# A three-layer network kernel on one core: the idle products at the stage seams are taken out

## The chip, the core and the metric

The kernel runs on one core of a Trainium2 chip. The engines are named as the profile names them: PE is TensorE (the products), DVE is VectorE, ACT is ScalarE, POOL is GpSimd, SP is SyncE, which issues most DMAs. The metric is the device time of one execution in microseconds.

## What is computed

One sequence of 512 tokens with 1024 features goes through three layers in float32:

```
x = x + ssd_gla_layer(rms_norm(x)); x = x + swiglu(rms_norm(x))     # layer 1: state space mixer and gated linear attention
x = x + mla_layer(rms_norm(x));     x = x + swiglu(rms_norm(x))     # layer 2: latent attention
h = rmsnorm(x)                                                      # layer 3
x = x + (sigmoid(gate_a) * (o_hg @ w_branch_hg) + sigmoid(gate_b) * (o_ret @ w_branch_ret)) @ w_out
x = x + peer_ffn(rmsnorm(x))                                        # 8 heads choose 16 of 16384 experts for each token
return rmsnorm(x)
```

`swiglu` is `(silu(h @ w_gate) * (h @ w_up)) @ w_down` with 2816 hidden features. `o_hg` and `o_ret` are the outputs of a gated recurrence (HGRN2) and of a retention layer. `peer_ffn` scores all experts by product keys, and adds `g * gelu(u_e . x) * v_e` for each chosen expert.

## The kernel before, in words

The work is one long row of stages, and in nearly all of them PE multiplies a weight matrix by the activations. Activations lie transposed in SBUF as 8 tiles of 128 features by 512 tokens (`c.xT`). Float32 precision is had from three products: each operand is split in a high half in the faster format `F32R` and a low half, the rest. ACT makes the high half by a copy, DVE or POOL the low half by a subtraction, and `passes` (L430 to L434) does high by high, high by low and low by high. Weights come in pieces of 128 by 1024 through a ring of two slots (four in the expert stage): SP loads, ACT writes `w_hi`, POOL writes `w_lo`, PE uses it. Every engine has its own instruction order, and semaphores with counted values tie them (`Tally`).

A stage is written in a block of its own, or shares one with its neighbour. At the end of a block the engines meet; PE then waits until DVE has opened the next stage (the semaphore increment at L661 in `linear_block`, at L2085 in `swiglu`). Such a place is called a seam here. Most seams hold a root mean square norm: PE sums squares (`root`, L290 on, uses the sum), ACT takes the logarithm and the exponential, and in the next stage the class `Normal` (L307 on) makes the eight parts of the normalised activations in turn. DVE multiplies (L357), ACT copies the high half (L337), and DVE (L362, parts 0, 1, 2, 4, 6) or POOL (L348, parts 3, 5, 7) makes the low half. POOL also splits one weight piece in front of them (L344). PE takes part k when its low half is there (`normal.ready`): three products a part where one output tile is made at a time (`linear_block`), six where two are made together (`swiglu` at L2068 and `first_latents` at L2349 on), two in the first pass of the expert stage (L3465, L3466).

At these seams the kernel has idle products. They multiply a constant by a constant into a bank of PSUM that is overwritten at once, and nobody waits for them:

```
285 def occupy(c, pe, bank, n):
287     for _ in range(n):
288         pe.matmul(c.ps[:, bank, 0:3 * P], c.ident, c.basic[:, 0:3 * P], start=True, stop=True)
```

They stand at the start of a stage with a norm or with halves of its own to make (L646, L2068, L2349, L3517: three each), at the end of a token-major layer (`linear_tokens`, L795: three), before the last sum of squares in `direct_attention` (L1726: four), behind two layers of 16 output tiles (L651, through the argument `rest`: four each), and before the expert sums (L3570: six). Over the run these are 63 products. In the seams behind the two layers with `rest` they are followed by the next stage's three.

The last stage (`peer_stream`, L3073 on) has two halves. In the first, 128 pieces of expert inputs are multiplied by the activations (L3465 to L3469), and meanwhile DVE and POOL treat the gates. In the second, `add(n, i)` adds 128 pieces of expert outputs: for each piece SP loads weights and two inputs (L3183, L3203, L3205), ACT and DVE make the halves of the multiplied weights (L3379, L3699; L3695 multiplies) and of the expert rows (L3275, L3704), and PE does 18 products into six banks. DVE also adds the first 128 tokens' own rows (L3713), which POOL gathers (L3418).

Of the kernel before, what the change touches and what calls it, by code (L numbers as in the profile page):

```python
# [283 lines left out]

def occupy(c, pe, bank, n):

    for _ in range(n):
        pe.matmul(c.ps[:, bank, 0:3 * P], c.ident, c.basic[:, 0:3 * P], start=True, stop=True)

def root(c, act, width):
# [93 lines left out]
def first_pieces(w):  # L385

    return [w[m, :, :] for m in range(min(2, w.shape[0]))]
# [49 lines left out]
def linear(c, w, kt, nb, hi, lo, dst, add=False, src=None, then=None, beside=None, root_of=None, normal=None,  # L437
           width=D, more=None, ends=None, loads=(), rest=0, whole=None, run=None, head=True, tail=True, tokens_next=False):

    with ExitStack() as ctx:
        linear_block(c, ctx, w, kt, nb, hi, lo, dst, add, src, then, beside, root_of,
                     Normal(c, ctx, normal, width, whole, ends, (hi, lo)) if normal else None, more, loads, rest,
                     run, head, tail, tokens_next)
# [6 lines left out]

def linear_block(c, ctx, w, kt, nb, hi, lo, dst, add, src, then, beside, root_of, normal, more, extra=(), rest=0,
                 run=None, head=True, tail=True, tokens_next=False):
# [49 lines left out]
    with opened(c, run) as block:  # L507
# [112 lines left out]
        @block.tensor  # L620
        def _(pe):
            if head:
                pe.sem_inc(c.piece_free.sem, 2)

            def one(i, r, q, m, s, first=False):
                pe.wait_ge(c.lo_done.sem, c.lo_done.at(3) + m)
                if q == 0:

                    pe.wait_ge(c.bank_free.sem, c.bank_free.at(1) + i)
                if not head and q == 1 and m == 1:  # L630
                    pe.wait_ge(c.bank_free.sem, c.bank_free.at(2))
                for k in range(pt):
                    at = slice(k * P, (k + 1) * P)
                    if first and normal:
                        normal.ready(pe, k)
                    elif first:

                        pe.wait_ge(c.dve_done.sem, c.dve_done.at(k + 1))
                    mm = passes(pe, c.ps[:, r, :], half(c.w_hi, s)[:, at], half(c.w_lo, s)[:, at],
                                hi(q * pt + k), lo(q * pt + k), q == 0 and k == 0, q == np_ - 1 and k == pt - 1)  # L640
                mm.then_inc(c.piece_free.sem, 1)
                if more:
                    more[1](pe, i)
            if src or normal:
                pe.wait_ge(c.bank_free.sem, c.bank_free.at(1))
                occupy(c, pe, 0, 3)  # L646
                one(0, 0, 0, 0, 0, first=True)
            pieces(one, None if root_of or more else pe.Fori, 1 if src or normal else 0)
            if rest:
                pe.wait_ge(c.bank_free.sem, c.bank_free.at(1 + nb))  # L650
                occupy(c, pe, nb % 2, rest)  # L651
            if root_of:
                pe.wait_ge(squares_added.sem, squares_added.at(nb - 2))
                pe.matmul(c.ps[:, RS, :], c.ones, square_sum[:], start=True, stop=False)
                pe.wait_ge(c.squared.sem, c.squared.at(nb))
                pe.matmul(c.ps[:, RS, :], c.ones, sq[:, (nb - 1) % 4, :], start=False, stop=True).then_inc(c.summed.sem, 1)
# [51 lines left out]
def linear_tokens(c, w, kt, nb, hi, lo, dst, beside=None, run=None, head=True):  # L708
# [29 lines left out]
    with opened(c, run) as block:  # L738
# [35 lines left out]
        def _(pe):  # L774
# [19 lines left out]
            pe.wait_ge(c.bank_free.sem, c.bank_free.at(1 + nb * NCH))  # L794
            occupy(c, pe, 4 * flip, 3)  # L795

# [840 lines left out]
def direct_attention(c, x, v, out, gate, then):  # L1637
# [7 lines left out]
    with ExitStack() as ctx:  # L1645
# [8 lines left out]
        with nc.Block() as block:  # L1654
# [7 lines left out]
            def _(pe):  # L1662
# [55 lines left out]
                for h in range(H):  # L1718
# [5 lines left out]
                    if h:  # L1724
                        sum_squares(h - 1)
                occupy(c, pe, 3, 4)  # L1726
                sum_squares(H - 1)
# [238 lines left out]
def swiglu(c, layer, then):  # L1966
# [11 lines left out]
    with c.nc.Block() as run, ExitStack() as ctx:  # L1978
        hid_hi = c.sb(ctx, f"hid_hi{layer}", [P, HT, T], F32R)
        hid_lo = c.sb(ctx, f"hid_lo{layer}", [P, HT, T], F32R)  # L1980
        with ExitStack() as inner:
# [3 lines left out]
            with nullcontext(run) as block:  # L1985
# [64 lines left out]
                def _(pe):  # L2050
# [16 lines left out]
                    pe.wait_ge(c.bank_free.sem, c.bank_free.at(1))  # L2067
                    occupy(c, pe, 0, 3)  # L2068
                    for k in range(DT):
# [52 lines left out]
def latent_attention(c, then):  # L2122
# [15 lines left out]
    with ExitStack() as ctx:  # L2138
# [44 lines left out]
        with nc.Block() as block:  # L2183
# [43 lines left out]
            def _(pe):  # L2227
# [120 lines left out]
                def first_latents():  # L2348
                    occupy(c, pe, 0, 3)  # L2349
                    pe.wait_ge(c.lo_done.sem, split_at(0))  # L2350
# [575 lines left out]
def mix2(c):  # L2926
# [3 lines left out]
    with ExitStack() as outer:  # L2930
# [39 lines left out]
        with ExitStack() as ctx:  # L2970
# [10 lines left out]
            with ExitStack() as inner:  # L2981
                g = c.sb(inner, "g_ret", [P, 16, T])
                gated = GatedNorm(c, inner, lambda t: qk[:, t, :], lambda t: g[:, t, :])
                linear(c, d["w_ret_g"], DT, 16, hh, hl, g, beside=(gated.vector, gated.scalar),
                       more=(lambda sp, m: None, gated.tensor, gated.gpsimd), then=first_pieces(d["w_branch_ret0"]),
                       rest=4)
                gated.close()
            y_ret = c.sb(ctx, "y_ret", [P, DT, T])
            with ExitStack() as inner:
# [11 lines left out]
            linear(c, d["w_gates"], DT, 16, hh, hl, qk, beside=(merge.vector, merge.scalar), then=first_pieces(d["w_out_2"]),  # L3001
                   rest=4, run=block, head=False)
            run.close()
# [69 lines left out]
def peer_stream(c, hh, hl, out):  # L3073
# [6 lines left out]
    with ExitStack() as ctx:  # L3080
# [86 lines left out]
        with nc.Block() as block:  # L3167
# [287 lines left out]
            def _(pe):  # L3455
# [50 lines left out]
                def gates(g):  # L3506
# [9 lines left out]
                    mm.then_inc(gate_mm.sem, 1)  # L3516
                occupy(c, pe, 0, 3)  # L3517
                for m in range(NQ):
# [35 lines left out]
                def add(n, i, first=False):  # L3554
# [14 lines left out]
                    mm.then_inc(c.mm_done.sem, 1)  # L3569
                occupy(c, pe, SUM_BANK[0], 6)  # L3570
                for i in range(4):
# [323 lines left out]
```

## Time and profile before

| | us |
|---|---|
| median of 3 runs | 3753.21 (3751.49 to 3753.91) |
| the profiled execution | 3751.39 |
| its span, from first to last instruction | 3749.2 |

The profile is one execution. The trace gives each instruction's start and length; the length of a product contains a tail in which the next one already runs, so the distance of two starts tells what one costs.
### The profile page before, as it was taken

Reading aid. Unit: us, or ns where it says so; the run is one execution under the profiler, and the core shown is the slowest. Engines: PE = TensorE matmul, PEld = TensorE weight load, DVE = VectorE, ACT = ScalarE, POOL = GpSimd, SP = SyncE. Lnnn points to the kernel's source line nnn. Section 1 sums busy time; section 2 is a strip of 40 time slices with the busy share of each in tenths; the row PEclk is TensorE's granted clock in tenths of the full one; section 3 lists DMA queues with packets and bytes.
Section 4 is the critical chain, followed back from the end, with each engine's and each line's share of the span. In section 5 each row is a group of like instructions: output and inputs, shape, how many; then the busy total and the mean of one; then the engine's idle time right before and its main releaser. Section 6 shows DMA issues by size and latency. Waiting matters only on the chain. (4 is left out here: it accounts for less than half of the span.)

```text
span 3749.2 us, 50283 instructions
## 1 busy us (share of the span) xinstructions
PE 3610.9 (96%) x17367; PEld 2990.4 (80%) x17367; DVE 1963.0 (52%) x3524; ACT 1384.3 (37%) x2161; POOL 1624.1 (43%) x838
## 2 busy tenths in 40 slices
PE   8899899998999999998899999999999999999999
PEld 6668678886677888787687777779999999888887
DVE  6825333204653330227516122458899992788777
ACT  3333332224653222231221332333348994333333
POOL 4444354344105444441344344445786776342221
PEclk9999999999999999999999999999999999999999
DMA  5122132222002222230132122224778997999997
GB/s 172 34 92 92 43 98 95 95 96 83 23 23 97 95 90 94 84 95 23 42 115 85 51 79 85 90 99 142 267 244 298 380 378 288 364 361 357 344 343 254
DMA packets 275168, 580.19 MB, mean 155 GB/s; under 512 B 119712, under 2 KB 153888, under 8 KB 273616
## 3 DMA queue, kind: packets, MB, share of 16 engines
q1 hardware_dynamic: 238160, 444.07, 35.9%
q0 software_dynamic: 36864, 134.23, 10.1%
q8 instruction: 87, 1.43, 0.2%
q14 instruction: 57, 0.47, 0.0%
HBM read 523.66 MB, written 54.56 MB: 154 GB/s over the span
## 5 line engine op out<-in xcount | busy, mean ns | idle before, releaser
L432 PE MATMUL ps<-h_hi,w_hi 128*128 128x512 f32 x1880 | 744.3, 396 | 21.3 <-DVE h_lo L362 11.0
L433 PE MATMUL ps<-h_lo,w_hi 128*128 128x512 f32 x1880 | 736.5, 392 | 0.0
L434 PE MATMUL ps<-h_hi,w_lo 128*128 128x512 f32 x1880 | 736.4, 392 | 0.0
L594 POOL TENSOR_TENSOR w_lo<-ring,w_hi 128x1024 fp32r<-128x1024 f32 (+1 forms) x173 | 445.9, 2578 | 637.0 <-ACT w_hi L559 637.0
L559 ACT CAST w_hi<-ring 128x1024 fp32r<-128x1024 f32 (+1 forms) x173 | 191.5, 1107 | 734.5 <-PE ps L434 728.9
L432 PEld LDWEIGHTS ps<-h_hi,w_hi 128*128 128x128 f32 x1880 | 355.8, 189 | 112.3 <-DVE h_lo L362 15.4
L3414 POOL TENSOR_TENSOR w_lo<-ring,w_hi 128x1024 fp32r<-128x1024 f32 x142 | 359.1, 2533 | 151.6 <-ACT w_hi L3275 150.5
L434 PEld LDWEIGHTS ps<-h_hi,w_lo 128*128 128x128 f32 x1880 | 355.8, 189 | 75.0
L433 PEld LDWEIGHTS ps<-h_lo,w_hi 128*128 128x128 f32 x1880 | 355.8, 189 | 74.9 <-issue 2.2
L3275 ACT CAST w_hi<-ring 128x1024 fp32r<-128x1024 f32 x270 | 282.2, 1045 | 351.7 <-PE ps L434 269.0
L3465 PE MATMUL ps<-h_hi,w_hi 128*128 128x384 f32 (+1 forms) x1152 | 399.9, 347 | 3.8 <-DVE h_lo L362 3.1
L3466 PE MATMUL ps<-h_lo,w_hi 128*128 128x384 f32 (+1 forms) x1152 | 394.7, 343 | 0.0
L3418 POOL DMA_INDIRECT xT<-in_expert_v,row_index x128 | 150.0, 1172 | 377.7 <-DVE ps L3713 363.1
L432 PE MATMUL ps<-w_hi,one_hots 128*128 128x512 f32 x768 | 303.8, 396 | 1.1 <-DVE one_hots L3699 1.1
L434 PE MATMUL ps<-w_hi,one_hots 128*128 128x512 f32 x768 | 303.4, 395 | 0.0
L433 PE MATMUL ps<-w_lo,one_hots 128*128 128x512 f32 x768 | 303.4, 395 | 0.0
L2035 POOL TENSOR_TENSOR w_lo<-ring,w_hi 128x1024 fp32r<-128x1024 f32 x84 | 201.9, 2404 | 227.6 <-ACT w_hi L2008 227.5
L675 DVE TENSOR_TENSOR xT<-xT,ps 128x512 f32 x48 | 33.0, 687 | 383.4 <-PE ps L434 383.4
L3469 PE MATMUL ps<-h_hi,w_lo 128*128 128x384 f32 (+1 forms) x1152 | 230.6, 341 | 1.8 <-POOL w_lo L3414 1.8
L3465 PEld LDWEIGHTS ps<-h_hi,w_hi 128*128 128x128 f32 x1152 | 217.6, 189 | 11.7 <-DVE h_lo L362 4.0
L3466 PEld LDWEIGHTS ps<-h_lo,w_hi 128*128 128x128 f32 x1152 | 218.0, 189 | 4.5
L3469 PEld LDWEIGHTS ps<-h_hi,w_lo 128*128 128x128 f32 x1152 | 203.9, 188 | 7.7 <-POOL w_lo L3414 2.5
(430 smaller groups left out, 6661.3 us busy)
## 6 DMA issues: line engine op xcount, KB each, us to landing
ring<-in_expert_u SPq DMA_DIRECT2D x128, 512.0 KB, 4.8
ring<-in_expert_v SPq DMA_DIRECT2D x128, 512.0 KB, 5.9
ring<-in_w_gate_up SPq DMA_DIRECT2D x88, 512.0 KB, 3.6
acts<-expert_gelu SPq DMA_DIRECT2D x128, 192.0 KB, 4.2
gates<-peer_region SPq DMA_DIRECT2D x48, 512.0 KB, 8.1
peer_region<-acts SPq DMA_DIRECT2D x128, 192.0 KB, 4.8
peer_region<-gates SPq DMA_DIRECT2D x128, 192.0 KB, 5.8
ring<-in_w_down SPq DMA_DIRECT2D x32, 704.0 KB, 4.1
```

Of the source, the lines that this page charges most:

```text
L432: pe.matmul(out, w_hi, x_hi, start=start, stop=False)
L433: pe.matmul(out, w_hi, x_lo, start=False, stop=False)
L434: return pe.matmul(out, w_lo, x_hi, start=False, stop=stop)
L559: act.copy(half(c.w_hi, s), raw(s)).then_inc(c.hi_done.sem, 1)
L594: pool.tensor_tensor(half(c.w_lo, s), raw(s), half(c.w_hi, s).bitcast(F32), ALU.subtract).then_inc(c.lo_done.sem, 1)
L2035: pool.tensor_tensor(c.w_lo[:, at], c.ring[:, u * SLOT:u * SLOT + D], c.w_hi[:, at].bitcast(F32), ALU.subtract).then_inc(c.lo_done.sem, 1)
L3275: act.copy(at_slot(c.w_hi, i), at_slot(c.ring, i)).then_inc(c.hi_done.sem, 1)
L3414: pool.tensor_tensor(at_slot(c.w_lo, i), at_slot(c.ring, i), at_slot(c.w_hi, i).bitcast(F32), ALU.subtract).then_inc(c.lo_done.sem, 1)
L3418: pool.indirect_dma_start(rows[:, j % 4, :], None, table, bass.IndirectOffsetOnAxis(ap=row_at[:, j:j + 1], axis=0)).then_inc(row_loaded[j ...
L3465: pe.matmul(to, c.w_hi[:, at[k]], hh(k)[:, x0:T], start=k == 0, stop=False)
L3466: pe.matmul(to, c.w_hi[:, at[k]], hl(k)[:, x0:T], start=False, stop=False)
L3469: mm = pe.matmul(to, c.w_lo[:, at[k]], hh(k)[:, x0:T], start=False, stop=k == DT - 1)
```

## The change

All calls of `occupy` go, with the function and the argument `rest` that carried a count to one of them. Waits, loads and every other instruction stay as they are.

```diff
-def occupy(c, pe, bank, n):
-
-    for _ in range(n):
-        pe.matmul(c.ps[:, bank, 0:3 * P], c.ident, c.basic[:, 0:3 * P], start=True, stop=True)
...
             if src or normal:
                 pe.wait_ge(c.bank_free.sem, c.bank_free.at(1))
-                occupy(c, pe, 0, 3)
                 one(0, 0, 0, 0, 0, first=True)
             pieces(one, None if root_of or more else pe.Fori, 1 if src or normal else 0)
-            if rest:
-                pe.wait_ge(c.bank_free.sem, c.bank_free.at(1 + nb))
-                occupy(c, pe, nb % 2, rest)
...
             pe.wait_ge(c.bank_free.sem, c.bank_free.at(1 + nb * NCH))
-            occupy(c, pe, 4 * flip, 3)
...
                     if h:
                         sum_squares(h - 1)
-                occupy(c, pe, 3, 4)
                 sum_squares(H - 1)
...
                     pe.wait_ge(c.bank_free.sem, c.bank_free.at(1))
-                    occupy(c, pe, 0, 3)
                     for k in range(DT):
...
                 def first_latents():
-                    occupy(c, pe, 0, 3)
                     pe.wait_ge(c.lo_done.sem, split_at(0))
...
-                occupy(c, pe, 0, 3)
                 for m in range(NQ):
...
-                occupy(c, pe, SUM_BANK[0], 6)
                 for i in range(4):
                     add(i, i, first=i == 0)
```

With `rest` the wait in front of its products goes too; two calls had `rest=4`.

## Rows read from the trace of the kernel before

**Rows 1.** The page's first lines, and the view of the cores
```profile
span 3749.2 us, 50283 instructions
...
PE 3610.9 (96%) x17367; PEld 2990.4 (80%) x17367; DVE 1963.0 (52%) x3524; ACT 1384.3 (37%) x2161; POOL 1624.1 (43%) x838
...
core 0: 3749.2 us, clock 0.989
```

**Rows 2.** The idle products' line: records, and what ended the idle time before them
```profile
L288 PE MATMUL ps<-basic x126: 484/486/1007, 17.2 to 3202.2; 128*128 128x384 f32 x126
...
  DVEq L661: 34.6, 16
```

**Rows 3.** Timeline of PE, 14 to 30 us: start, length, what, idle before
```profile
17.19 2.17 PE L288 MATMUL ps<-basic 128*128 128x384 f32 x6 [1.83 <-DVEq L661]
...
22.53 0.50 PE L432 MATMUL ps<-h_hi,w_hi 128*128 128x512 f32 x1 [2.19 <-DVE h_lo L362]
22.86 0.39 PE L433 MATMUL ps<-h_lo,w_hi 128*128 128x512 f32 x1
23.09 0.40 PE L434 MATMUL ps<-h_hi,w_lo 128*128 128x512 f32 x1
...
26.21 0.63 PE L434 MATMUL ps<-h_hi,w_lo 128*128 128x512 f32 x1
26.64 0.63 PE L432 MATMUL ps<-h_hi,w_hi 128*128 128x512 f32 x1
```

**Rows 4.** Timeline of DVE and of POOL in the same stretch
```profile
20.04 2.43 DVE L362 TENSOR_TENSOR h_lo<-conv_y,h_hi 128x512 fp32r<-128x512 f32 x1
...
27.81 1.29 POOL L348 TENSOR_TENSOR h_lo<-conv_y,h_hi 128x512 fp32r<-128x512 f32 x1 [0.74 <-ACT h_hi L337]
```

**Rows 5.** Stretches of 12 us; PEclk is the third number from the end
```profile
17.19:29.19 12.00, 9.28 (x27) 5.59 (x28) 10.41 (x13) 5.75 (x9) 6.23 (x4) 0.86 0.32 90
...
860.63:872.63 12.00, 8.34 (x22) 5.47 (x23) 10.49 (x10) 6.51 (x8) 5.83 (x2) 0.78 0.55 193
...
1528.50:1540.50 12.00, 8.44 (x28) 4.55 (x28) 10.41 (x13) 5.75 (x9) 6.23 (x4) 1.00 0.38 120
...
2402.24:2414.24 12.00, 10.89 (x43) 8.00 (x44) 5.59 (x9) 7.90 (x12) 4.91 (x2) 1.00 0.30 83
2454.03:2466.03 12.00, 8.20 (x20) 4.17 (x20) 10.54 (x14) 6.69 (x10) 6.17 (x5) 0.81 0.59 225
```

**Rows 6.** Timelines of POOL at 1166 us and of PE at 869 us
```profile
1166.03 1.29 POOL L348 TENSOR_TENSOR h_lo<-whole,h_hi 128x512 fp32r<-128x512 f32 x1 [0.75 <-ACT h_hi L337]
...
869.52 0.50 PE L432 MATMUL ps<-h_hi,w_hi 128*128 128x512 f32 x1 [3.65 <-DVE h_lo L362]
```

**Rows 7.** Timelines behind 2402 us: DVE and PE
```profile
2404.00 2.50 DVE L666 TENSOR_TENSOR h_lo<-y_hg,h_hi 128x512 fp32r<-128x512 f32 x4 [2.43 <-ACT h_hi L553]
...
2404.84 0.47 PE L432 MATMUL ps<-h_hi,w_hi 128*128 128x512 f32 x1 [0.42 <-DVE h_lo L666]
...
2411.20 0.50 PE L432 MATMUL ps<-h_hi,w_hi 128*128 128x512 f32 x1 [0.68 <-POOL w_lo L594]
```

**Rows 8.** Timeline at the end of the gated attention, 424 to 429 us
```profile
424.24 2.74 PE L288 MATMUL ps<-basic 128*128 128x384 f32 x8
...
427.19 1.98 PE L1714 MATMUL ps<-sq,basic 128*128 128x512 f32 x4 [0.21 <-ACT proj_gla L1748]
```

**Rows 9.** Timelines at the start of the expert sums: DVE and PE
```profile
3197.53 0.56 DVE L3699 TENSOR_TENSOR one_hots<-peer_region,one_hots 128x384 fp32r<-128x384 f32 x1 [0.98 <-ACT one_hots L3379]
...
3198.63 4.03 PE L288 MATMUL ps<-basic 128*128 128x384 f32 x12
...
3217.12 0.56 DVE L3695 TENSOR_TENSOR peer_region<-peer_region 128x384 f32<-128x384 f32 x1 [8.60 <-DMA peer_region<-gates]
...
3220.53 0.50 PE L432 MATMUL ps<-w_hi,one_hots 128*128 128x512 f32 x1 [1.07 <-DVE one_hots L3699]
```

**Rows 10.** Timeline of PE at the start of the retention scores
```profile
2057.19 1.10 PE L2811 MATMUL ps<-qk_ret 128*128 128x512 f32 x2 [1.11 <-PEq L2978]
```

More of the change, by code:

```diff
@@ L437, in linear @@
 def linear(c, w, kt, nb, hi, lo, dst, add=False, src=None, then=None, beside=None, root_of=None, normal=None,
-           width=D, more=None, ends=None, loads=(), rest=0, whole=None, run=None, head=True, tail=True, tokens_next=False):
+           width=D, more=None, ends=None, loads=(), whole=None, run=None, head=True, tail=True, tokens_next=False):
     with ExitStack() as ctx:
         linear_block(c, ctx, w, kt, nb, hi, lo, dst, add, src, then, beside, root_of,
-                     Normal(c, ctx, normal, width, whole, ends, (hi, lo)) if normal else None, more, loads, rest,
+                     Normal(c, ctx, normal, width, whole, ends, (hi, lo)) if normal else None, more, loads,
                      run, head, tail, tokens_next)
@@ L453, in opened, with linear_block @@
     return nullcontext(run) if run is not None else c.nc.Block()
-def linear_block(c, ctx, w, kt, nb, hi, lo, dst, add, src, then, beside, root_of, normal, more, extra=(), rest=0,
+def linear_block(c, ctx, w, kt, nb, hi, lo, dst, add, src, then, beside, root_of, normal, more, extra=(),
                  run=None, head=True, tail=True, tokens_next=False):
@@ L2984, in mix2 @@
                 linear(c, d["w_ret_g"], DT, 16, hh, hl, g, beside=(gated.vector, gated.scalar),
-                       more=(lambda sp, m: None, gated.tensor, gated.gpsimd), then=first_pieces(d["w_branch_ret0"]),
-                       rest=4)
+                       more=(lambda sp, m: None, gated.tensor, gated.gpsimd), then=first_pieces(d["w_branch_ret0"]))
                 gated.close()
@@ L3001, in mix2 @@
             linear(c, d["w_gates"], DT, 16, hh, hl, qk, beside=(merge.vector, merge.scalar), then=first_pieces(d["w_out_2"]),
-                   rest=4, run=block, head=False)
+                   run=block, head=False)
             run.close()
```

## The prediction

> **What bounds the kernel now.** I began with the page's busy shares: TensorE (PE) is busy 96% of a span of 3749.2 us, and its mean granted clock is 0.989 [rows 1]. So nearly all of the time is a stream of products, and what the edit can move is either time in that stream or the clock at which the stream runs. A mean of 0.989 between the levels of 2.4 and 1.2 GHz means 2 x 0.011 x 3749 = 82 us at the lower level already, in the kernel that has the idle products.
>
> Then I asked for the line of the idle products. The trace has 126 of them as records, two for each of 63 calls, and in most cases PE had been waiting before the first, for the signal with which VectorE (DVE) opens the next stage [rows 2]. One record takes 0.32 us of PE at 2.4 GHz: twelve in a row last 4.03 us, the last of them 0.49 with its tail [rows 2, 9], and (4.03 - 0.49) / 11 = 0.32; six take 1.9 us. All 126 together are 126 x 0.32 = 41 us of PE time.
>
> Next came the timeline of one seam, on PE and on the engines that feed it. The six records end at 17.19 + 2.17 = 19.36; then PE does the three products of part 0 and stands 2.19 us until part 1 of the normalised activations is there [rows 3]. DVE makes that part in 2.43 us, and the eighth part is finished by GpSimd (POOL) at 27.81 + 1.29 = 29.10 [rows 4]. The starts on PE show the clock too: 22.86 to 23.09 is 0.23 us a product, 26.21 to 26.64 is 0.43 us, at the lower level [rows 3]. So the clock fell here, products or no products, after PE had idled around them. A view by stretches says where else: over the 12 us from a seam's first idle product the granted clock is 0.86 in this seam and 0.78 at 861, but 1.00 at 1528 and at 2402; of twelve such rows, of which the first and the last stand among the five shown, nine are below 1.00 [rows 5]. 0.86 over 12 us is 2 x 0.14 x 12 = 3.4 us at the lower level.
>
> **The change, part by part.** It removes 63 products at 17 places, and the two waits for a free bank that stood in front of the `rest` products; what follows those is the end of a block, which waits for DVE and ACT anyway. It adds nothing: no wait, no DMA, no work on another engine. No semaphore hangs on them, so no engine is let go sooner or later by their absence as such. Three prices matter: PE time given back, the first real products of a stage which may start sooner, and the clock.
>
> *PE time given back.* In sixteen of the places the products lie inside a wait of PE. At the seam at 17.19 the product that decides is the one at 22.53 [rows 3]; starting part 0 earlier by a few tenths moves nothing, as part 1 comes when DVE has it [rows 4]. At the end of the gated attention PE waits another 0.21 us for ScalarE (ACT) after eight records [rows 8]; before the retention scores it waits 1.11 us for the stage to open [rows 10]; at 2404.84 it waits 0.42 us for the first half made by DVE [rows 7]. I take 0, between 0 and -0.1 us at each.
>
> The seventeenth is different. The six products before the expert sums stand on PE's path: the multiplied weights of the first piece were finished at 3197.53 + 0.56 = 3198.09, yet the sums come behind twelve records that begin at 3198.63 [rows 9]. Without them the sums start 12 x 0.32 = 3.9 us sooner. But 18 us later PE waits 1.07 us for piece 4, whose weights DVE could not multiply until their DMA had landed, after 8.60 us of waiting, at 3217.12 [rows 9]. Nothing in that chain comes from PE's sums, so piece 4 still starts at 3220.53, and the 3.9 us turn into a wait: the gap becomes 1.07 + 3.9 = 5.0 us. Between a gain of 3.9 us (if the transfers came sooner too) and 0, I take 0.
>
> *The clock.* After a gap of 3.65 us at 869.52 in another stage [rows 6] the clock was low, and also after 2.19 us at 22.53 [rows 3]. Without the products PE is idle for their 1.9 us on top of what it waits before and behind them, 1.83 and 2.19 us in the seam shown [rows 3], so I expect the clock to fall at almost every seam, and sooner. Whether it costs anything depends on who is late:
>
> - Eight seams with three products a part, two in the last (17, 196, 431, 1529, 1826, 2206, 2259, 2454). Parts 1 to 7 come over 22.47 to 29.10, 1.1 us each [rows 4]; three products take 0.68 us at the upper level and 1.29 us at the lower. All seven parts at the lower level would end at 22.53 + 7 x 1.29 = 31.5 instead of 29.10 + 0.68 = 29.8: 1.7 us late. But a low stretch that begins sooner ends sooner, and the one in the trace cost nothing since it was over before the eighth part. Between 0 and 1.7 us; nearest to the row, 0.15 each: +1.2.
> - Three seams with six products a part (489, 861, 1156). Six take 1.36 us, eight times that is 10.9, and in the last of these seams the eighth part is there at 1166.03 + 1.29 = 1167.32 [rows 6], some 12 us after the seam's start, and PE has no slack from part 2 on. Each added 3.4 us stretch costs half of it, 1.7 us. At 861 the clock is at 0.78 already [rows 5], and a wait of 3.65 us [rows 6] hides low time. Between 0 and 3.4 each; I take 1.7 + 1.7 + 0.1 = +3.5.
> - The seam at 2402, where parts are made at 2.50 / 4 = 0.62 us [rows 7] against 0.68 us on PE, so PE is the bound at once. Its clock was 1.00 [rows 5]. One low stretch costs 1.7 us, and 0.68 us of waiting for POOL at 2411.20 [rows 7] can absorb some. Between 0 and 3.4: +1.5.
> - Three ends of token-major layers (386, 1711, 2054). At 2054 PE-bound score products follow at once, at the others small products that wait for DVE. Between 0 and 1.7 each: +1.3 at 2054, +0.3 for the two others.
> - The gated attention's end. Four sum products follow at 427.19 [rows 8]; they take 1.98 us, some 1.8 without the tail, which doubles if they run low. The clock may also fall only after them. Between 0 and 1.8: +0.5.
> - The expert sums. After the 5 us gap PE, which has no further wait there, runs low for 3.4 to 6 us: +1.7 to +3.1. I take +2.0.
>
> Sum: 1.2 + 3.5 + 1.5 + 1.6 + 0.5 + 2.0 = 10.3 us. The profiled execution took 3751.39 us, its span and 2.2 us around it; the median of the runs is 3753.21 us, 1.8 us above it. Added to the median: **3763.5 us**, +0.27%.
>
> On the page of the Trainium skill "TensorE: Matmul & The Clock Gate", section "HAM oscillation — how this bites in real kernels", the price of a throttled stretch is its length times one half. By that rule the 82 us of before cost 41 us, and any added low time is paid by half in full, which is the second case below. The seam at 17.19 speaks against paying it everywhere: there 3.4 us low cost nothing.
>
> **Rivals.** A measurement of this kernel can tell about 0.2%, 7.5 us, from no change: below 3745.7 is faster, above 3760.7 slower.
>
> *The full price.* PE comes out of each seam with a backlog, so low time is never hidden. One extra stretch of 3.4 us at 17 places costs 17 x 1.7 = 29 us: 3782 us. For it: PE is 96% busy. Against: the wait for parts in most seams. Chance 0.08.
>
> *The products do little.* In nine of the twelve stage starts the trace shows lower clock with the products in; then their absence only moves the low stretch forward, under the wait. Left would be the expert sums and one or two seams, +3 us: 3756 us. Against: three stage starts are at 1.00 today, 1528 and 2402 among them [rows 5], and the wait in front of piece 4 grows by more than it was long. Chance 0.27.
>
> *Faster.* The mechanism is the six products at 3198.63. It decides if piece 4 starts before 3220.53 in the changed kernel, that is, if the transfers are not what holds it. Then 3.9 us are kept, no gap forms, and with the rest hidden the time is 3753.2 - 3.9 = 3749.3 us. For it: those are the only products on the path. Against: the 8.60 us wait for the DMA. Chance 0.05. To reach 0.2% much more would have to be on the path, up to all 41 us, which the waits in [rows 2] rule out.
>
> That the edit doesn't do what it says is hardly possible: either the 126 records are gone or not.
>
> **The numbers.** The forecast's case has 0.60; its own range is 3757 to 3772, from the lower ends of the double seams and the sums to twice their values, and nine tenths of it lies above 3760.7. With the full price, 0.54 + 0.08 = 0.62 slower. Within 0.2%: 0.06 + 0.26 + 0.04 = 0.36. Faster by over 0.2%: 0.02. The range reaches from 3753, which takes in most of the second rival, to 3775, which leaves out the full price and most of the faster case: 3753 to 3775.
>
> **What would show it.** No record of the idle products; mean clock down from 0.989 to about 0.98; a low stretch in the 12 us after 1528, 2402 and 2054; the eighth part's products in a seam like the first still starting within 0.5 us of the part; from the seam at 1156 the block of 48 products 1 to 2 us longer; the first expert sum 0.1 us after the last projection, a gap of about 5 us before piece 4, and the lower level right after it. The prediction is wrong if the gap before piece 4 keeps its 1 us, if the mean clock stays at 0.989, or if stretches of low clock show up with PE's backlog behind every seam.

## The result, and the profile after

| | before | after |
|---|---|---|
| median, us (8 runs each) | 3751.74 (3748.88 to 3753.91) | 3761.88 (3759.53 to 3768.26) |
| the profiled execution, us | 3751.39 | 3768.26 |

The ratio is 1.0032, with a 95% interval of 1.0022 to 1.0043: without the idle products the kernel is 10 us slower. The forecast was +10.3 us, to 3763.5, from a median of 3753.21 us in three runs; in eight runs the kernel before has 3751.74, so the measured +10.1 us ends at 3761.9. Of the kernel after, three of the eight executions took 3767 to 3768 us and five 3759.5 to 3762.3, and the profiled one is the longest. The page's first lines and the view of the cores, of the kernel after:

```profile
span 3766.1 us, 50042 instructions
...
PE 3591.5 (95%) x17241; PEld 2987.5 (79%) x17241; DVE 1957.8 (52%) x3524; ACT 1382.1 (37%) x2161; POOL 1619.3 (43%) x838
...
core 0: 3766.1 us, clock 0.976
```

PE is busy 19 us less than in [rows 1], and the span is 17 us longer in this execution. The mean clock went from 0.989 to 0.976: 2 x 0.024 x 3766 = 181 us at the lower level, where there were 82. A hundred more microseconds at half speed would be 50 us if nothing hid them; the median paid 10.

The first seam, on PE's timeline (start, length, what, idle before):

```profile
19.38 0.76 PE L426 MATMUL ps<-h_hi,w_hi 128*128 128x512 f32 x1 [4.06 <-DVE h_lo L356]
...
22.50 0.79 PE L426 MATMUL ps<-h_hi,w_hi 128*128 128x512 f32 x1 [1.50 <-DVE h_lo L356]
...
26.61 0.63 PE L426 MATMUL ps<-h_hi,w_hi 128*128 128x512 f32 x1
...
29.44 0.39 PE L426 MATMUL ps<-h_hi,w_hi 128*128 128x512 f32 x1
```

and POOL's last half there:

```profile
27.79 1.28 POOL L342 TENSOR_TENSOR h_lo<-conv_y,h_hi 128x512 fp32r<-128x512 f32 x1 [0.76 <-ACT h_hi L331]
```

Against [rows 3] the products run at the lower level from the first one on: 19.38 is 0.76 long, and 22.50 is 0.79 long, not 0.50. Part 7 is ready at 27.79 + 1.28 = 29.07, and its products start at 29.44, where the forecast allowed 0.5 us behind the part. The low stretch is three times as long as before (0.57 over these 12 us is 10.3 us, against 3.4), since it began sooner; it ended about half a microsecond later, but still before part 7. The whole seam costs 0.2 us. Stretches of 12 us from a stage start on, with PEclk the third number from the end, answering to [rows 5]:

```profile
17.15:29.15 12.00, 8.27 (x20) 5.71 (x21) 10.42 (x13) 5.75 (x9) 6.22 (x4) 0.57 0.27 90
...
865.76:877.76 12.00, 4.40 (x10) 3.04 (x11) 8.91 (x8) 6.61 (x8) 4.69 (x2) 0.59 0.42 138
...
1534.46:1546.46 12.00, 6.52 (x14) 4.33 (x15) 10.10 (x13) 6.68 (x11) 4.93 (x3) 0.60 0.40 122
...
2417.10:2429.10 12.00, 9.69 (x32) 7.82 (x33) 5.59 (x9) 7.55 (x12) 2.93 (x2) 0.72 0.31 86
...
2472.20:2484.20 12.00, 9.68 (x23) 5.52 (x24) 8.38 (x11) 5.36 (x9) 8.37 (x5) 0.57 0.48 194
```

No stage start is at 1.00 any more, 2259 among those not shown: 1528 (now 1534) went from 1.00 to 0.60, 2402 (now 2417) from 1.00 to 0.72. The waits in front of the places where products were taken out, on PE's timeline, for [rows 7, 8, 10]:

```profile
431.20 3.56 PE L1703 MATMUL ps<-sq,basic 128*128 128x512 f32 x4 [2.79 <-ACT proj_gla L1736]
...
496.64 0.77 PE L426 MATMUL ps<-h_hi,w_hi 128*128 128x512 f32 x1 [3.98 <-DVE h_lo L356]
...
1722.08 2.26 PE L1311 MATMUL ps<-proj_hg 128*128 128x128 f32 x9 [3.05 <-PEq L2939]
...
2069.95 2.90 PE L2797 MATMUL ps<-qk_ret 128*128 128x512 f32 x3 [3.05 <-PEq L2964]
...
2419.41 0.76 PE L426 MATMUL ps<-h_hi,w_hi 128*128 128x512 f32 x1 [6.65 <-DVE h_lo L656]
```

The gated attention's four sum products show the price most plainly. They started as soon as ACT let them, as before, but take 3.56 us instead of 1.98: behind the 2.79 us that four idle products had filled, PE ran at the lower level. It does not do so each time: e5 below has the same wait there and its sum products take 1.98 us. At 2070 three score products take 2.90 us where two took 1.10. At 2419 the gap is 6.65 us; it was two waits of 1.47 and 0.42 us around products. The expert sums, for [rows 9], on PE, on DVE, and over the 12 us that hold the gap:

```profile
3213.10 0.47 PE L426 MATMUL ps<-w_hi,one_hots 128*128 128x512 f32 x1 [0.55 <-DVE one_hots L3682]
...
3235.15 0.80 PE L426 MATMUL ps<-w_hi,one_hots 128*128 128x512 f32 x1 [5.02 <-DVE one_hots L3682]
```

```profile
3231.74 0.56 DVE L3678 TENSOR_TENSOR peer_region<-peer_region 128x384 f32<-128x384 f32 x1 [9.29 <-DMA peer_region<-gates]
```

```profile
3230.00:3242.00 12.00, 6.98 (x21) 5.42 (x21) 10.26 (x13) 5.52 (x7) 5.01 (x3) 0.72 1.09 346
```

The sums start behind the projections after a wait of 0.55 us, and PE stands 5.02 us before piece 4, as worked out ahead (5.0). DVE waits 9.29 us for the transfer, 8.60 before. Then 0.72 over 12 us: 2 x 0.28 x 12 = 6.7 us at the lower level.

To see where time went, the products that both kernels have, all 17241 in the same order, were taken, and the time from the start of one to the start of another compared. Each row runs from the last product ahead of a seam to one in the dense part of the stage behind it, so that waits and idle products lie inside. Differences to the profile of before, in us, with the experiments told of below:

```
stage      before  after     e1     e3     e4     e5     e6     e7     e8    e10    e11
17          21.68  +0.17  -0.02  -0.03  +0.03  +0.11  +0.00  -0.01  +0.02  -0.00  -0.01
196         22.90  +0.02  -0.01  +0.02  -0.01  +0.02  -0.00  -0.00  +0.00  +0.42  +0.00
386         14.92  +1.39  -0.00  +0.00  +0.01  +0.00  +1.18  +0.02  +0.01  +1.58  +0.01
attention   12.34  +1.58  -0.01  -0.00  -0.00  +0.09  -0.01  +0.00  -0.00  -0.01  -0.01
431         23.60  +0.01  +0.06  +0.01  +0.02  -0.09  -0.00  +0.01  +0.01  +0.02  +0.05
489         30.28  +1.14  -0.01  +0.02  +2.20  -0.00  +1.67  -0.01  +2.49  +1.16  +0.27
861         30.13  +0.83  +0.77  -0.10  -0.21  -0.17  +1.12  -0.15  -1.54  +0.83  -1.55
1156        29.60  +0.31  +0.03  -1.17  +0.64  -0.73  +0.35  -1.15  -0.29  +0.32  -1.16
1529        25.41  +0.15  +0.01  +0.03  +0.01  +0.05  +0.17  -0.00  +0.01  +0.14  +0.01
1711        12.46  +1.65  -0.10  +0.52  -0.09  +1.99  +1.51  +0.41  -1.63  +1.76  -1.63
1826        27.39  +0.00  -0.00  +0.01  -0.00  +0.01  +0.00  -0.00  -0.01  +0.00  -0.01
2054        27.08  +1.42  +0.00  -0.00  -0.00  -0.00  +3.06  +0.00  +0.00  +2.96  +0.00
2206        31.95  -0.02  -0.02  +0.12  -0.03  -0.01  +0.56  +0.12  -0.02  +0.53  +0.17
2259        27.89  +0.42  +0.02  +0.01  +0.02  +0.01  +0.01  -0.00  +0.00  +0.02  -0.00
2402        30.99  +1.41  -0.00  +0.00  +0.01  +1.57  +0.48  +0.00  +0.03  +0.44  +0.00
2454        34.03  -0.82  -0.04  -0.98  +0.05  -0.73  -0.96  -0.97  +0.08  -0.93  -0.99
sums        43.97  +3.13  +1.81  -0.02  +0.15  -0.27  +2.78  -4.05  +2.57  -3.83  -4.77
1800-1822   22.56  +3.82  +0.01  +0.01  +0.01  +0.01  +0.01  +0.01  +0.01  +0.01  +0.01
3050-3100   49.99  -1.51  -2.44  -2.49  -2.44  -1.04  -2.14  -2.47  -2.72  -2.69  -2.13
```

Each column is one execution (e9 has -4.19 in the sums; e12 and e13 are told of below). The last two stages have no idle product in either kernel, and 861, 1156, 1711 and 2454 differ in kernels that leave them as they were. So do stretches that no kernel touches: from 999 to 1153 six of the thirteen other profiles are 2.4 to 2.6 us longer than that of before, e4 and e5 among them, and the rest are equal to it. A single reading of a stage carries up to 2.6 us of its own.

### The profile page after: what moved, and what is told of

It reads as the page before. It is cut to its first block and busy times, and to the rows that moved or that the text cites. A ratio compares the mean times of both kernels' runs of the same rounds, so it can differ in the third digit from the quotient of the medians.

```text
span 3766.1 us, 50042 instructions
## 1 busy us (share of the span) xinstructions
PE 3591.5 (95%) x17241; PEld 2987.5 (79%) x17241; DVE 1957.8 (52%) x3524; ACT 1382.1 (37%) x2161; POOL 1619.3 (43%) x838
## 3 DMA queue, kind: packets, MB, share of 16 engines
q0 software_dynamic: 36864, 134.23, 10.1%
## 5 line engine op out<-in xcount | busy, mean ns | idle before, releaser
L3403 POOL DMA_INDIRECT xT<-in_expert_v,row_index x128 | 142.2, 1111 | 388.6 <-DVE ps L3696 373.9
```

Source lines behind the costliest of these rows:

```text
L3403: pool.indirect_dma_start(rows[:, j % 4, :], None, table, bass.IndirectOffsetOnAxis(ap=row_at[:, j:j + 1], axis=0)).then_inc(row_loaded[j ...
```

## The experiments

Each kernel was timed in five rounds; an interval is some 3 us to either side. The theory is the forecast's: the products' work holds the clock, and what low clock costs depends on who is late. The rivals are those of the prediction: the full price, the products do little, the six before the sums stand on the path.

**e1_sums_only.** The kernel before without the last group:

```diff
-                occupy(c, pe, SUM_BANK[0], 6)
                 for i in range(4):
                     add(i, i, first=i == 0)
```

> Only the six idle products before the expert sums are out; the other 57 stay. Forecast's theory (clock, and waits that hide it): the sums start 3.9 us sooner, piece 4 still waits for its transfer, the gap before it grows from 1.1 to 5 us, the clock is at the lower level right behind it, and the whole is 1 to 3 us slower than before. Rival (products on the path): 3.9 us faster, gap below 2 us. Rival (the products do little): within 1 us, gap 5 us but clock at 1.00.

Measured: 3752.06 us against 3749.80, ratio 1.0003 (0.9994 to 1.0012). By the median +2.3, but the interval runs from -2.3 to +4.5 us, so the times alone exclude only the rival's -3.9. The profile decides the rest. PE's timeline, and the 12 us behind the gap:

```profile
3199.42 0.47 PE L432 MATMUL ps<-w_hi,one_hots 128*128 128x512 f32 x1 [0.21 <-DVE one_hots L3698]
...
3220.69 0.79 PE L432 MATMUL ps<-w_hi,one_hots 128*128 128x512 f32 x1 [4.23 <-DVE one_hots L3698]
```

```profile
3220.70:3232.70 12.00, 12.00 (x43) 9.58 (x44) 11.16 (x14) 5.00 (x7) 5.29 (x4) 0.81 1.08 361
```

The sums start at once, the gap grew from 1.07 to 4.23 us, and 0.81 over 12 us is 4.6 us at the lower level, where [rows 9] had none. Over the stage this is +1.8 us. The start was won and lost again, and the low stretch came on top.

**e3_single_seams.** No idle products at the eight stage starts with one output tile at a time:

```diff
             if src or normal:
                 pe.wait_ge(c.bank_free.sem, c.bank_free.at(1))
-                occupy(c, pe, 0, 3)
+                if src:
+                    occupy(c, pe, 0, 3)
                 one(0, 0, 0, 0, 0, first=True)
...
-                occupy(c, pe, 0, 3)
                 for m in range(NQ):
```

> Idle products are out at the eight stage starts with a norm and one output tile at a time (17, 196, 431, 1529, 1826, 2206, 2259, 2454 us); all others stay. Forecast's theory: the clock is low for about twice as long there, but most of it lies beside the waits for the parts: +1 us, between 0 and +4 us. Rival (full price, low time never hidden): the added low time by half, 8 times 1.7 to 3.4 us, 14 to 27 us.

Measured: 3749.50 us against 3749.80, ratio 0.9997 (0.9988 to 1.0006). That is -4.5 to +2.2 us by the interval. The 12 us from the start of the stage at 2259 on, where before had no low time:

```profile
2259.30:2271.30 12.00, 9.30 (x28) 6.05 (x29) 9.20 (x12) 5.67 (x10) 6.23 (x4) 0.72 0.27 86
```

0.72 is 6.7 us at the lower level, and the stage takes 27.90 us instead of 27.89. So low time beside the wait for the parts is free, and half of it (3.4 us) would have been the full price of this one seam alone. The full price, 14 to 27 us over all eight, is out.

**e4_double_seams.** No idle products at 489, 861 and 1156:

```diff
                     pe.wait_ge(c.bank_free.sem, c.bank_free.at(1))
-                    occupy(c, pe, 0, 3)
...
                 def first_latents():
-                    occupy(c, pe, 0, 3)
```

> Idle products are out at the three stage starts that make two tiles together (489, 861, 1156 us); all others stay. Forecast's theory: no slack on TensorE there, +3.5 us (the trace of the whole change shows +2.3, +0.8 and +0.2 at the three). Rival (the products do little): within 1 us. Rival (full price): half of all added low time, 5 us or more.

Measured: 3753.85 us against 3749.80, ratio 1.0008 (0.9999 to 1.0017): +4.1 us by the median for three seams, where e3's eight gave -0.3. The two intervals overlap, and this one still holds no change, so the profile has to carry it. The stage at 489, now from 492.6 on:

```profile
492.60:504.60 12.00, 9.09 (x24) 6.74 (x25) 10.15 (x13) 7.43 (x11) 6.23 (x4) 0.57 0.30 89
```

0.57 is 10.3 us at the lower level, where before had 2.9 by 0.88, and the stage is 2.2 us longer. Half of the added 7.4 us would be 3.7. PE waits twice at the start of this stage, as in the kernel after (3.98 and 0.96 us), and not again: with six products a part it is behind from then on. The other two seams read -0.2 and +0.6 us here. 861 is no longer than before, with nothing to be seen of a price.

**e5_ends.** The remaining places: token-major ends, the gated attention, `rest`, and the stage start at 2402:

```diff
             if src or normal:
                 pe.wait_ge(c.bank_free.sem, c.bank_free.at(1))
-                occupy(c, pe, 0, 3)
+                if normal:
+                    occupy(c, pe, 0, 3)
                 one(0, 0, 0, 0, 0, first=True)
...
-            if rest:
-                pe.wait_ge(c.bank_free.sem, c.bank_free.at(1 + nb))
-                occupy(c, pe, nb % 2, rest)
...
-            occupy(c, pe, 4 * flip, 3)
...
-                occupy(c, pe, 3, 4)
                 sum_squares(H - 1)
```

> Idle products are out at the three ends of token-major layers, before the last sum of squares of the gated attention, behind the two layers with rest=4 and at the start of the output layer at 2402 us; stage starts with a norm and the expert sums keep theirs. Forecast's theory: +3.6 us, 1.6 at the token-major ends, 0.5 at the attention, 1.5 at 2402; after the trace of the whole change rather +7 (1.4 + 1.6 at 386 and 431, 1.7 at 1721, 1.4 at 2069, 1.4 at 2417). Rival (the products do little): within 1 us.

Measured: 3756.01 us against 3749.80, ratio 1.0015 (1.0006 to 1.0024), +6.2 us. Two of its stretches of 12 us:

```profile
1720.00:1732.00 12.00, 9.72 (x55) 9.29 (x54) 8.90 (x16) 1.05 (x1) 3.76 (x2) 0.72 0.26 87
...
2410.00:2422.00 12.00, 10.39 (x35) 8.37 (x36) 5.59 (x9) 6.90 (x12) 3.46 (x2) 0.72 0.30 90
```

0.72 at 1720 and at 2410; the two stages are 2.0 and 1.6 us longer. In this execution 386, 2054 and the attention cost nothing, while in the profile of after they cost 1.4, 1.4 and 1.6. The attention's sum products, on PE's timeline:

```profile
432.14 1.98 PE L1711 MATMUL ps<-sq,basic 128*128 128x512 f32 x4 [2.79 <-ACT proj_gla L1744]
```

The wait is the 2.79 us of the kernel after, and the products run at the upper level. At 2054 it is the same: PE waits 3.05 us in both kernels, and the stage costs 1.4 us in one and nothing in the other. So the same wait costs in one execution and not in the next, and one profile does not settle the price of an end.

The four parts add up to 2.3 - 0.3 + 4.1 + 6.2 = 12.3 us by the medians, against 10.1 for all together, equal within their intervals.

**e6_narrow.** All 63 products in place, but 16 columns wide:

```diff
-        pe.matmul(c.ps[:, bank, 0:3 * P], c.ident, c.basic[:, 0:3 * P], start=True, stop=True)
+        pe.matmul(c.ps[:, bank, 0:16], c.ident, c.basic[:, 0:16], start=True, stop=True)
```

> All 63 idle products stay in their places, but multiply 16 columns instead of 384. If what held the clock is the work that they give the array, this is as slow as the change: +8 to +12 us, mean clock about 0.977. Rival (it is enough that some product runs at the seam, or that the queue is kept awake): within 2 us of before, clock 0.989.

Measured: 3761.22 us against 3750.95, ratio 1.0027 (1.0016 to 1.0038). Its line of idle products, and its clock:

```profile
L288 PE MATMUL ps<-basic x126: 177/263/374, 16.7 to 3208.9; 128*128 128x16 f32 x126
```

```profile
core 0: 3761.1 us, clock 0.978
```

All 126 records are there, weights are loaded for each, semaphores, queue and the place of all other instructions are as before, and the time is that of the kernel with none (3761.88). Only 368 of the 384 columns are missing. So what the idle products are worth lies in the work that they give the array, and nothing else that they do, such as keeping PE's queue filled, kept the mean clock at 0.989.

**e7_late_copy.** As e1, and the two transfers for the last step go behind the loop on SP:

```diff
-                sp.dma_start(x_tok, d["xs"]).then_inc(final_loaded.sem, 16)
-                sp.dma_start(final_w, d["final_rows"]).then_inc(final_loaded.sem, 16)
                 with sp.Fori(1, NB // 4) as p:
                     for i in range(4):
                         down(p * 4 + i, i)
                         inputs(p * 4 + i, i)
+                sp.dma_start(x_tok, d["xs"]).then_inc(final_loaded.sem, 16)
+                sp.dma_start(final_w, d["final_rows"]).then_inc(final_loaded.sem, 16)
```

> As e1_sums_only, and the 2.5 MB that the very last step needs (tokens and final weights) are requested after the expert sums' loop instead of at its start. If these transfers are what holds piece 4, the 8.6 us wait and the gap before piece 4 go, the clock stays at 1.00, and both the 3.9 us and the old gap of 1.1 us are kept: 5 us faster than before, 7 us faster than e1. Rival (transfers are short in this stage whatever their order): a gap comes elsewhere, at the end above all, and the time is that of before or more.

Measured: 3744.18 us against 3750.95, ratio 0.9982 (0.9973 to 0.9991), 3 to 10 us faster than before. DVE's timeline at the inputs of piece 4, and the clock:

```profile
3209.53 0.56 DVE L3694 TENSOR_TENSOR peer_region<-peer_region 128x384 f32<-128x384 f32 x1 [0.29 <-DMA peer_region<-gates]
```

```profile
core 0: 3742.1 us, clock 0.992
```

The wait that was 8.60 us is 0.29 us, PE has no gap before piece 4 any more, and the stage is 4.05 us shorter than before, 5.9 shorter than in e1. It fits the other half of the reading of [rows 9], that the six idle products stood on the path and the late transfer hid it; but this kernel changes both at once, and e12 takes them apart.

**e8_second_gap.** More idle products at the double seams, between part 0 and part 1:

```diff
                             if k == DT - 1:
                                 mm.then_inc(c.piece_free.sem, 1)
+                        if k == 0:
+                            occupy(c, pe, 5, 2)
...
                             if k == DT - 1:
                                 mm.then_inc(made.sem, 1)
+                        if k == 0:
+                            occupy(c, pe, 3, 5)
```

> As before, with idle products added between part 0 and part 1 at the three seams that make two tiles together (two at 489 and 1156, five at 861). Forecast's theory: they lie inside the waits of 0.5 to 3.7 us there, one low stretch less at each of 861 and 1156 (and perhaps at 489): 1 to 4 us faster than before. Rival (products between the parts delay the real ones, and the clock falls anyway after the wait for the stage to open): 0 to 2 us slower.

Measured: 3755.27 us against 3750.95, ratio 1.0008 (0.9999 to 1.0017): not faster, and the rival is nearer. PE's timeline at 499:

```profile
498.87 0.50 PE L432 MATMUL ps<-h_hi,w_hi 128*128 128x512 f32 x1 [1.69 <-POOL w_lo L344]
...
499.73 2.76 PE L288 MATMUL ps<-basic 128*128 128x384 f32 x4
...
501.72 1.20 PE L432 MATMUL ps<-h_hi,w_hi 128*128 128x512 f32 x1
```

The wait of this stage lies before the second tile of part 0 (1.69 us, for POOL's weight half), and the products had been put behind it, in front of work that was ready. They ran into the low stretch besides, at 2.76 us for two. At 861, where the wait does lie between the parts, five products cost nothing and the stage is 1.54 us shorter. So the idea holds for that seam, and the placing of the other two was wrong. A part of this profile's excess is not the edit's: the sums read +2.57 us with nothing changed there. The transfer came later in this execution (DVE waited 9.62 us for it), and PE's timeline before piece 4 is:

```profile
3226.77 0.76 PE L432 MATMUL ps<-w_hi,one_hots 128*128 128x512 f32 x1 [2.10 <-DVE one_hots L3703]
```

A gap of 2.10 us, with the six idle products in place, and the lower level behind it (0.76, not 0.50 as in [rows 9]). e9_both put e7 and e8 together:

> The edits of e7_late_copy and e8_second_gap together. They lie in different stages and should add: 6 to 9 us faster than before. Rival: as in those two, 0.

It took 3744.65 us against 3750.95, ratio 0.9985 (0.9976 to 0.9994), as e7 alone; the two do not add.

**e10_out_late_copy.** The whole change with e7's late transfers.

> The whole change, all 63 idle products out, with the late transfers of e7_late_copy. Without a wait for piece 4 the sixth part of the change's price (gap and low clock behind it, about 3 us) goes and the stage keeps its 5 us: 8 us faster than the change, 3754 us, so about 2 us slower than before and 10 us slower than e7_late_copy. Rival (the late transfers help only while the clock stays up): 3760 us or more.

Measured: 3755.86 us against 3750.35, ratio 1.0017 (1.0008 to 1.0026). Between e7 and this kernel lie the 57 other products: -6.8 us against +5.5 us, each against its own runs of before, 12.3 us. It is 3.5 us more than expected. e3, e4 and e5, which take the same 57 out in three parts, add up to 10.0 us, so the two ways agree within their intervals. The gain in the sums is the same in both (-4.05 and -3.83), so the late transfers help as much with the clock lower elsewhere; the rival of this run, 3760 us or more, is touched only by the upper end of the interval.

**e11_gap_filled.** e7 with two products before the wait for the second tile and five at 861:

```diff
                             if k == 0 and m == 1:
+                                occupy(c, pe, 5, 2)
                                 pe.wait_ge(c.lo_done.sem, c.lo_done.at(4))
...
+                        if k == 0:
+                            occupy(c, pe, 3, 5)
```

> e7_late_copy with two idle products in the right place at 489 and 1156, in front of the wait for the second weight tile, where e8 had put them behind it, and the five at 861 that in e8 lay inside a 3.7 us wait. Forecast's theory: no delay, one low stretch less at 861 and at times at 489 and 1156: 1 to 4 us faster than e7_late_copy, 3740 to 3743 us. Rival (the clock falls for the wait ahead of the stage, whatever follows): same as e7_late_copy within 1 us.

Measured: 3744.64 us against 3750.35, ratio 0.9988 (0.9979 to 0.9997), while e7 had 0.9982. The 1.55 us at 861 are there again in the profile; the total shows no gain over e7 (3744.18), which is what the rival forecast. Open: the products that would be needed to keep the clock up at every seam were not tried one by one.

**e12_copy_only and e13_late_copy_again.** The late transfers alone, with all 63 products in place, beside a second run of e7's kernel; against e7, e12 has one line more:

```diff
+                occupy(c, pe, SUM_BANK[0], 6)
                 for i in range(4):
                     add(i, i, first=i == 0)
```

> The kernel before with nothing but the two late transfers (the token copy and the final rows requested on SP behind the loop of the expert pieces); all 63 idle products stay, the six before the expert sums too. e7_late_copy, which also lacks these six, had 0.9982, 6.8 us under before. Theory (the six stand on PE's path once the transfer for piece 4 is not late): only the 1.07 us gap before piece 4 goes, and the 3.9 us of the six stay in front of the sums; the stage of the sums is 1 to 1.5 us shorter than before and not 4, and the time 3748 to 3750.5 against 3750.5, 1.0000 to 0.9993. Rival (the late transfers alone bring the gain, through the DMA queues or what follows the sums, and the six are not on the path): 3743 to 3745, 0.9980 to 0.9987, and the stage of the sums some 4 us shorter with the six in it.

> The kernel of e7_late_copy once more, on the same chip and beside the same runs as e12_copy_only, to set the six products against their absence with all else equal. Theory: 3 to 4 us less than e12_copy_only, at 0.9980 to 0.9987 of before. Rival (the six are not on the path): within 1 us of e12_copy_only.

Measured: e12 took 3748.11 us and e13 3745.86, against 3750.69; ratios 0.9994 (0.9985 to 1.0003) and 0.9986 (0.9977 to 0.9995). The difference of 2.3 us points the way of the theory, but the two intervals overlap. The stage of the sums is plainer: against before it is 1.34 us shorter in e12, and 5.20 in e13 (4.05 in e7). PE's timeline in e12, at the sums:

```profile
3193.27 4.03 PE L288 MATMUL ps<-basic 128*128 128x384 f32 x12
...
3196.84 0.69 PE L432 MATMUL ps<-w_hi,one_hots 128*128 128x512 f32 x1
```

DVE's, at the weights of the first piece and the inputs of piece 4:

```profile
3193.44 0.56 DVE L3699 TENSOR_TENSOR one_hots<-peer_region,one_hots 128x384 fp32r<-128x384 f32 x1 [1.25 <-ACT one_hots L3379]
...
3207.58 0.56 DVE L3695 TENSOR_TENSOR peer_region<-peer_region 128x384 f32<-128x384 f32 x1 [0.64 <-DMA peer_region<-gates]
```

The twelve records begin at 3193.27, and the first sum starts behind them at 3196.84, though the weights it needs were multiplied at 3193.44 + 0.56 = 3194.00. The inputs come 0.64 us late instead of 8.60, so PE's gap is gone, as in e7; what remains between the two kernels is the six products, 4.05 - 1.34 = 2.7 us by e7's profile and 3.9 by e13's, against 3.9 worked out ahead. So they stand on the path once the transfer is in time, and in the kernel before the transfer hid that.

## Why the prediction was right

The direction, the size and the mechanism held: no idle time was given back at the seams, what was lost is clock, and it cost where PE was late. The total is closer than its terms. To judge a term better than by one profile, the profiles in which a seam's idle products are gone or narrow (after, e6, e10 and the experiment on that group) can be set against all those that have them as before, by their means (all fourteen profiles, e9, e12 and e13 read as in the table above; for the seams with two tiles without e8, e9 and e11, which add products there; for the sums without the kernels with late transfers). In us:

```
term                        forecast   profile of after   mean without less mean with
eight single seams             1.2          -0.1                   0.1
three double seams             3.5           2.3                   3.3
start at 2402                  1.5           1.4                   1.0
three token-major ends         1.6           4.5                   5.0
gated attention                0.5           1.6                   0.4
expert sums                    2.0           3.1                   2.1
together                      10.3          12.8                  11.9
```

Two terms were off: the single seams were put 1 us too high, the token-major ends 3 us too low. The interval of the measured difference is 8 to 16 us and holds all three sums; that the forecast came within 0.2 us of the 10.1 is partly luck.

- *Idle time given back: 0 at sixteen places.* Right in the seam shown: the next real product starts when its part is there, at 22.50 against 22.53.
- *The six before the sums: earlier start, same piece 4, gap of 5 us.* Right in the gap (5.02) and in the transfer as its cause, which e12 shows by moving the transfer alone. The sums start some 3 us sooner, not 3.9: without the products PE waits 0.55 us for the multiplied weights (0.21 in e1), which had been read as ready.
- *Low clock behind that gap, +2.0.* +3.1 in the profile of after, +1.8 in e1: about right.
- *Eight single seams, +1.2.* Too large. They sum to -0.1 in the profile of after, and at 2259 e3's 6.7 us of low time were free. At 196 the mean clock over 12 us went from 0.74 to 0.57, 10.3 us of low time, and the stage is as long as it was. The forecast's reason, that a low stretch which begins sooner ends sooner, held in e3 but not in the first seam of after; there the stretch was over before the last part all the same.
- *Three double seams, +3.5.* Right in sum, +4.1 by e4's median. The split was not: 861 was put at 0.1 and reads +0.8 to +1.1 in after, e6 and e10 but -0.2 in e4 and +0.8 in e1, which has its products; 1156 was to be 1 to 2 us longer and is 0.3 longer than in before's profile, 1.1 by the means.
- *The start at 2402, +1.5.* +1.4 and +1.6, and +0.5 in e6 and e10.
- *Three token-major ends, +1.6.* The worst-sized term: 1.4 + 1.7 + 1.4 = 4.5 in the profile of after. The forecast had named the 2054 stage alone as bound by PE at once. At 1711 the small products take longer too (sixteen of them 2.8 us in e5, 2.0 before), and DVE, which works on what they make, waits 1.0 us for the second and the third group of them, where before it waited 0.2 and 0.4. So they are on the path as well. For 386 the same is likely, not shown. 2054 reads 0 in e5 and 3.0 in e6 and e10.
- *The gated attention, +0.5.* +1.6 where the clock fell before the sum products, 0 in e5, e6 and e10 where it did not. The forecast had allowed for both.

Of the rivals, the full price is out by the time itself (10 us, not 29) and by e3. That the products do little, +3 us, lies below the measured interval. The faster case fails with the early transfers, and e7 shows the very mechanism that it named once they come in time.

The rule of the Trainium skill ("TensorE: Matmul & The Clock Gate", section "HAM oscillation — how this bites in real kernels"), half of the throttled time, gives as an estimate 50 us for the added 99 us. The trace disagrees: 17 us in that execution, 10 in the median. Single places came near to half, as the gated attention did in after, with 1.6 us for the 3.4 us at the lower level around its sum products; where PE had waits left in the stretch it was less, down to nothing.

## What to carry to other kernels

Idle products in front of a wait are worth their place when what comes behind the wait is bound by TensorE: the start of a dense stage, a short chain of sums that others wait for. Where the next operands come slower than the throttled engine can use them, they gain nothing. Price each place by who is late in the 10 us behind it, not by how busy the engine is overall, and by more than one profile, since the same wait may cost in one execution and not in another; and ask of each group whether it stands inside a wait or on the path, since a late transfer further on can hide that it is on the path.

## What was not expected

Low stretches come in stages that nobody touched. In the profile of after one fell into the forget-gated attention:

```profile
1823.60:1833.80 10.20, 8.23 (x35) 7.83 (x36) 1.52 (x5) 1.34 (x3) 1.27 (x1) 0.50 0.00 0
```

10.2 us at the lower level over the chain of state sums there, and the stretch from 1800 to 1822 is 3.8 us longer; no other profile has it. The stage's waits are the same as before, it only runs 9 us later. In the same way there is a low stretch behind a wait of 1.77 us at 88 us, and the stretch from 85 to 110 us is 2.3 us longer in this execution; in the others it differs by at most 0.8:

```profile
88.19 0.50 PE L426 MATMUL ps<-h_hi,w_hi 128*128 128x512 f32 x1 [1.77 <-POOL w_lo L588]
```

These two may be what sets the three longer executions of the change apart from the five shorter ones, but only one profile of the eight exists, so this is not shown. The stretch from 3050 to 3100 is 1.0 to 2.9 us shorter in all thirteen other profiles, since a low stretch of before's profile, at 3062, is missing in all of them: a single profile of before was not free of this either.
